# RMS norms of a two-layer decoder trunk on one core: from blocks between the matmul stages to steps streamed into them, the residual update on VectorE alone

## What is computed

```python
def rms_norm(x, g):
    y = x * lax.rsqrt(jnp.mean(x * x, axis=-1, keepdims=True) + RMS_EPS)
    return y * g

def decoder_layer(x, mem_kv, past, lp, rel_bias):
    g = lp['norm_g']
    mix, st = mixer_block(rms_norm(x, g[0]), lp, rel_bias, past)
    x = x + rms_norm(mix, g[1])
    x = x + rms_norm(cross_attention(rms_norm(x, g[2]), mem_kv, lp['w_xq'], lp['w_xo']), g[3])
    x = x + rms_norm(swiglu(rms_norm(x, g[4]), lp['w_ffn_in'], lp['w_ffn_out']), g[5])
    return x, st
```

## Time and profile before

| | |
|---|---|
| time, median of 3 executions | 3706.91 us (3703.59 to 3714.84) |
| profiled execution, its own time | 3719.7 us |
| its span, core 0 | 3717.9 us |
| mean granted TensorE clock | 0.812 |
| TensorE matmuls busy | 2937.5 us (79%) |
| TensorE weight loads busy | 2710.8 us (73%) |
| VectorE busy | 1452.8 us (39%) |
| ScalarE busy | 819.3 us (22%) |
| GpSimd busy | 353.1 us (9%) |
| HBM read / written | 385.95 / 19.55 MB, 109 GB/s over the span |

### The profile page before, as it was taken

One profiled execution on the slowest core, in us unless ns is written; L12 is line 12 of the kernel. 1 busy time (PEld: TensorE's weight loads), 2 busy tenths in 40 slices (PEclk: granted clock), 3 DMA queues, 4 the chain that ended last, 5 costly groups with the idle time before them and its releaser, 6 DMA issues. The chain is left out here.

```text
span 3717.9 us, 51710 instructions
## 1 busy us (share of the span) xinstructions
PE 2937.5 (79%) x19564; PEld 2710.8 (73%) x19564; DVE 1452.8 (39%) x3291; ACT 819.3 (22%) x1609; POOL 353.1 (9%) x344
## 2 busy tenths in 40 slices
PE   2798967469886797999939797865797867889997
PEld 1785656359885696999929665654697767879996
DVE  1225557315553313333122355762275332233322
ACT  0223311001222212222212232110122221222221
POOL 1000033230001001000010001324100010000000
PEclk8786789658996856999959778985598876689998
DMA  5221089443221401332113202956332140123331
GB/s 129 64 96 44 9 335 388 160 157 86 70 77 34 147 16 44 93 92 84 58 38 97 90 15 93 416 236 229 108 90 63 51 158 12 34 63 90 89 89 43
DMA packets 387293, 398.72 MB, mean 107 GB/s; under 512 B 47332, under 2 KB 350920, under 8 KB 370224
## 3 DMA queue, kind: packets, MB, share of 16 engines
q1 hardware_dynamic: 357888, 212.08, 19.6%
q0 software_dynamic: 29248, 184.63, 13.0%
HBM read 385.95 MB, written 19.55 MB: 109 GB/s over the span
## 5 line engine op out<-in xcount | busy, mean ns | idle before, releaser
L446 PE MATMUL pg<-act_hi,w_lo 128*128 128x260 f32 x3328 | 681.3, 286 | 116.4 <-PEq L149 43.7
L446 PE MATMUL pg<-act_hi,w_hi 128*128 128x260 f32 x3328 | 678.6, 286 | 0.0
L446 PE MATMUL pg<-act_lo,w_hi 128*128 128x260 f32 x3328 | 678.2, 286 | 0.0
L410 DVE TENSOR_TENSOR w_lo<-w_raw,w_hi 128x1024 fp32r<-128x1024 f32 x296 | 362.5, 1225 | 692.4 <-ACT w_hi L405 685.1
L446 PEld LDWEIGHTS pg<-act_hi,w_lo 128*128 128x128 f32 x3328 | 523.2, 192 | 121.4 <-issue 90.7
L446 PEld LDWEIGHTS pg<-act_hi,w_hi 128*128 128x128 f32 x3328 | 521.5, 191 | 0.0
L446 PEld LDWEIGHTS pg<-act_lo,w_hi 128*128 128x128 f32 x3328 | 520.8, 192 | 0.0
L405 ACT CAST w_hi<-w_raw 128x1024 fp32r<-128x1024 f32 x292 | 305.7, 1047 | 311.1 <-PE pg L446 140.1
L1240 PE MATMUL pg<-xt,w_raw 128*128 128x256 f32 x1024 | 243.7, 399 | 102.5 <-DVE xt L1303 102.5
L1240 PEld LDWEIGHTS pg<-xt,w_raw 128*128 128x128 f32 x1024 | 201.8, 200 | 141.6 <-DVE xt L1303 75.0
L1303 DVE STREAM_TRANSPOSE xt<-cache 128x256 f32<-128x256 f32 x512 | 180.8, 412 | 104.5 <-DMA cache<-in_cache_kv,gather_rows 104.3
(11 more groups left out here) (411 smaller groups left out, 3937.1 us busy)
## 6 DMA issues: line engine op xcount, KB each, us to landing
w_raw<-in_w_ffn_in SPq DMA_DIRECT2D x88, 512.0 KB, 3.8
w_raw<-in_w_in SPq DMA_DIRECT2D x80, 512.0 KB, 3.8
cmem<-in_cache_mem SPq DMA_DIRECT2D x16, 1024.0 KB, 14.2
w_raw<-in_w_ffn_out SPq DMA_DIRECT2D x32, 512.0 KB, 3.7
w_raw<-in_w_o SPq DMA_DIRECT2D x16, 512.0 KB, 3.7
w_raw<-in_w_xkv SPq DMA_DIRECT2D x16, 512.0 KB, 3.7
out_win_sample<-in_cache_win SPq DMA_DIRECT2D x2, 4088.0 KB
w_raw<-in_w_ffn_out SPq DMA_DIRECT2D x16, 384.0 KB, 3.2
```

What stands on the lines that cost most here:

```text
L410: e.tensor_tensor(w_lo[:, slot % 2, :], w_raw[:, slot, :], w_hi[:, slot % 2, :].bitcast(F32), ALU.subtract).then_inc(w_ready, 1)
L446: mm = e.matmul(pg[:, tslot, h, 0:wd], w[:, slot % 2, wk], x[:, k0 + k, at:at + wd], start=first and k == 0 and n == 0, stop=last and k == ...
```

## The change

- A norm's last factor, 1/rms of each token, is no longer multiplied into the operand of the next stage. It is a factor per column, so it is applied to the products: the operand is gain x `xT` alone, and VectorE multiplies each output tile by `rb`, a copy of the spread factor, when it empties PSUM (mixer, `ng`, merge gates, XQ, FFN-in).
- The squares for the norm after a sub-layer are made from PSUM as its output tiles come (`square_and_keep`), VectorE adds them up (`add_square`), and five small matmuls sum the total.
- The residual update (scale, add to `xT`, `act_lo` of the next operand) is done chunk by chunk on VectorE alone; ScalarE makes `act_hi` and the square of the new `xT`. GpSimd keeps the power.
- The next stage's first unit (XQ, FFN-in) runs chunk by chunk behind the update, and between its chunks TensorE sums the new squares with two float32 matmuls by `ones` (256 and 264 columns); the sums stand on all partitions, and `mean_square_dve` picks them off the diagonal.
- Norm 0 of layer 0 is done in a block ahead of the loop; for the next layer, the factor comes from the end of the FFN-out block. `norm_block` is gone.
- Blocks are merged: vector rows with mixer stage, WO with norms 1 and 2 and XQ, XO with norms 3 and 4 and FFN-in, FFN-out with norm 5. The ring's first four units are loaded ahead of the `cmp` weights. XKV moves into the LayerNorm block (units 44 to 51; OUT is 52, WO 60), with its operand prepared by VectorE in the gate stage's last three units. OUT and WO start when their operand's first chunk is split. Half of the `cache_mem` loads are issued in the WO block, half in the cross-attention block. A clear of the scope's semaphores moves to between cross attention and XO.

The diff, cut to what the prediction speaks of:

```diff
-U_MIX, U_MG, U_OUT, U_WO, U_XKV, U_XQ, U_XO, U_FI, U_FO, U_END = 0, 20, 44, 52, 60, 68, 72, 80, 124, 148
+U_MIX, U_MG, U_XKV, U_OUT, U_WO, U_XQ, U_XO, U_FI, U_FO, U_END = 0, 20, 44, 52, 60, 68, 72, 80, 124, 148
...
-        def norm_block(*norms):
...
+        def square_and_keep(e, n, u, m, dst, sq):
+            tile_done_(e, u)
+            if m >= 2:
+                e.wait_ge(acc_done, KC * n + m - 1)
+            elif n:
+                e.wait_ge(sq_used, KC * n)
+            e.activation(halves(sq[:, m % 2, :]), out_tile(m % 2), ACT.Square).then_inc(sq_ready, 1)
+            e.copy(halves(dst[:, m, :]), out_tile(m % 2)).then_inc(evac[m % 2], 1)
+        def add_square(e, n, m, sq, acc):
+            e.wait_ge(sq_ready, KC * n + m + 1)
+            if m == 0:
+                e.tensor_copy(acc, sq[:, 0, :]).then_inc(acc_done, 1)
+            else:
+                e.wait_ge(acc_done, KC * n + m)
+                e.tensor_tensor(acc, acc, sq[:, m % 2, :], ALU.add).then_inc(acc_done, 1)
...
+        def total_pe(e, n, acc):
+            e.wait_ge(acc_done, KC * n + KC)
+            for tt in range(5):
+                w = P if tt < 4 else NB
+                mm = e.matmul(pa[0][0:w, tt:tt + 1], acc[:, tt * P:tt * P + w], ones[:, 0:1], start=True, stop=True)
+            mm.then_inc(tot_mm, 1)
...
+        def keep_rb(e, n, i):
+            e.wait_ge(rstd_bc, i + 1)
+            e.copy(halves(rb[:]), pn[:, :, 0:HALF]).then_inc(rb_ready, 1)
...
+        def scaled_dve(e, n, c, B):
+            if c >= 4 and c % 2:
+                e.wait_ge(x_odd, 4 * n + (c - 4) // 2 + 1)
...
+            e.scalar_tensor_tensor(halves(B.t[:, c % 4, :]), halves(B.Y[:, c, :]), gain(2 * n + 1, c), pn[:, :, 0:HALF],
+                                   ALU.mult, ALU.mult).then_inc(t_ready, 1)
...
+        def add_x(e, n, c, B):
+            e.wait_ge(t_ready, KC * n + c + 1)
+            e.tensor_tensor(xT[:, c, :], xT[:, c, :], B.t[:, c % 4, :], ALU.add).then_inc(x_odd if c % 2 else x_even, 1)
...
+        def lo_dve(e, i, c):
+            e.wait_ge(hi_ready, KC * i + c + 1)
+            e.scalar_tensor_tensor(act_lo[:, c, :], xT[:, c, :], gain(2 * i, c), act_hi[:, c, :].bitcast(F32), ALU.mult, ALU.subtract
+                                   ).then_inc(lo_ready, 1)
...
+        def update_dve(e, n, B):
+            e.wait_ge(rstd_bc, 2 * n + 1)
+            scaled_dve(e, n, 0, B)
+            for c in range(KC):
+                if c + 1 < KC:
+                    scaled_dve(e, n, c + 1, B)
+                add_x(e, n, c, B)
+                if n < 2 and c:
+                    lo_dve(e, n + 1, c - 1)
+            if n < 2:
+                lo_dve(e, n + 1, KC - 1)
...
+        def update_act(e, n, B):
+            for c in range(KC):
+                e.wait_ge(x_odd if c % 2 else x_even, 4 * n + c // 2 + 1)
+                if n < 2:
+                    e.activation(act_hi[:, c, :], xT[:, c, :], ACT.Copy, scale=gain(2 * n + 2, c)).then_inc(hi_ready, 1)
+                if c >= 2:
+                    e.wait_ge(sq_used, KC * n + c - 1)
+                else:
+                    e.wait_ge(acc_done, KC * n + KC)
+                e.activation(B.sq[:, c % 2, :], xT[:, c, :], ACT.Square).then_inc(xsq_ready, 1)
...
+        def sum_squares(e, n, c, sq):
+            e.wait_ge(xsq_ready, KC * n + c + 1)
+            e.matmul(pa[0][:, 0:SPLIT], ones[:], sq[:, c % 2, 0:SPLIT], start=c == 0, stop=c == KC - 1)
+            e.matmul(pa[1][:, 0:TOK - SPLIT], ones[:], sq[:, c % 2, SPLIT:TOK], start=c == 0, stop=c == KC - 1).then_inc(sq_used, 1)
...
+        def mean_square_dve(e, n):
+            e.wait_ge(sq_used, KC * n + KC)
+            for t in range(5):
+                w = P if t < 4 else NB
+                src = pa[t // 2][0:w, (t % 2) * P:(t % 2) * P + w] if t < 4 else pa[1][0:NB, SPLIT:SPLIT + NB]
+                dve_chain(e, e.tensor_tensor_reduce(extract[0:w, 0:w], src, ident[0:w, 0:w], 1.0, 0.0, ALU.mult, ALU.add, ms[0:w, t:t + 1]))
+            e.tensor_scalar(ms[:], ms[:], 1.0 / D_MODEL, RMS_EPS, ALU.mult, ALU.add).then_inc(ms_ready, 1)
...
+        def first_stage(e, u0, n, i, sq):
+            await_(e, w_ready, u0 + 1)
+            await_(e, evac[0], u0 // 2)
+            for k in range(KC):
+                operand_ready(e, i, k)
+                wk = slice(k * P, (k + 1) * P)
+                for x, (w, v) in enumerate(((w_lo, act_hi), (w_hi, act_lo), (w_hi, act_hi))):
+                    for h in range(2):
+                        mm = e.matmul(pg[:, 0, h, 0:HALF], w[:, 0, wk], v[:, k, h * HALF:(h + 1) * HALF],
+                                      start=k == 0 and x == 0, stop=k == KC - 1 and x == 2)
+                if k == KC - 1:
+                    mm.then_inc(unit_done, 1)
+                sum_squares(e, n, k, sq)
...
+                        weights(e, U_MIX, RING, mix_parts)
...
-                        weights(e, U_MIX, RING, mix_parts)
...
+                            e.tensor_tensor(halves(to), out_tile(s % 2), halves(rb[:]), ALU.mult).then_inc(evac[s % 2], 1)
...
+                        e.tensor_tensor(halves(th[:]), pn[0:NG_W, :, 0:HALF], halves(rb[0:NG_W, :]), ALU.mult).then_inc(ng_sc, 1)
...
-            norm_block((0, xT, True))
...
+                        plain_stage(e, U_MIX, 20, (act_hi, act_lo), ready=lambda k: operand_ready(e, 0, k))
...
+                    e.dma_start(mem_f.rearrange("p c m -> p (c m)"), mem_dram.ap()).then_inc(mem_in, 16)
...
-                    tile_done_(e, U_MG + RING * j + s)
-                    e.activation(halves(G[:, bass.ds(RING * j + s, 1), :].rearrange("p o t -> p (o t)")), out_tile(s % 2), ACT.Tanh,
-                                 scale=0.5).then_inc(evac[s % 2], 1)
+                    u = RING * j + s
+                    await_(e, evac[s % 2], U_MG // 2 + 2 * j + s // 2 + 1)
+                    e.activation(G[:, bass.ds(u, 1), :].rearrange("p o t -> p (o t)"), sq_c[:, s % 2, :], ACT.Tanh, scale=0.5).then_inc(g_done, 1)
...
+                    if u >= 21:
+                        e.wait_ge(mem_in, 16)
+                        for c in range(3 * (u - 21), min(3 * (u - 21) + 3, KC)):
+                            link(e.tensor_scalar(mem_f[:, c, :], mem_f[:, c, :], vecs[:, V_MEM + c:V_MEM + c + 1], None, ALU.mult))
+                            link(e.tensor_copy(mem_hi[:, c, :], mem_f[:, c, :]))
+                            e.tensor_tensor(mem_lo[:, c, :], mem_f[:, c, :], mem_hi[:, c, :].bitcast(F32), ALU.subtract).then_inc(mem_set, 1)
+                    tile_done_(e, U_MG + u)
+                    if u >= 2:
+                        e.wait_ge(g_done, u - 1)
+                    e.tensor_tensor(halves(sq_c[:, s % 2, :]), out_tile(s % 2), halves(rb[:]), ALU.mult).then_inc(evac[s % 2], 1)
...
+                        e.wait_ge(mem_set, KC)
+                        unit(0)
+                        unit(1)
...
+                                if lead and s == 0:
+                                    e.wait_ge(op_lo, k + 1)
...
-                norm_block((1, Y, False), (2, xT, True))
...
+                        for m in range(KC):
+                            split_hi(e, U_WO + m + 1, (m + 1) % RING, landed(U_WO + m + 1))
+                            square_and_keep(e, 0, U_WO + m, m, bufs.Y, bufs.sq)
...
+                        split_hi(e, U_XQ + 1, 1, landed(U_XQ + 1))
+                        update_act(e, 0, bufs)
+                        split_hi(e, U_XQ + 2, 2, landed(U_XQ + 2))
+                        keep_rb(e, 0, 1)
...
+                            split_lo(e, U_WO + m + 1, (m + 1) % RING)
+                            add_square(e, 0, m, bufs.sq, bufs.acc)
+                        split_lo(e, U_XQ + 1, 1)
+                        total_dve(e, 0)
+                        diag_dve(e, 0, bufs.diag)
+                        update_dve(e, 0, bufs)
+                        mean_square_dve(e, 0)
+                        split_lo(e, U_XQ + 2, 2)
+                        diag_dve(e, 1, bufs.diag)
...
+                        total_pe(e, 0, bufs.acc)
+                        spread_pe(e, 0, bufs.diag)
+                        first_stage(e, U_XQ, 0, 1, bufs.sq)
+                        for s in range(1, XH):
+                            products(e, U_XQ + s, s, U_XQ // 2 + s // 2, s % 2, 0, KC, (act_hi, act_lo), True, True, (HALF, HALF))
+                            if s == 1:
+                                spread_pe(e, 1, bufs.diag)
...
-                norm_block((3, Y, False), (4, xT, True))
...
+                def fi_act(e, j, s):
+                    f = 2 * j + s // 2
+                    if s % 2 == 0:
+                        await_(e, evac[0], U_FI // 2 + f + 1)
+                        e.activation(thf[:, s // 2, :], gs[:, s // 2, :], ACT.Tanh, scale=0.5).then_inc(th_f, 1)
+                    else:
+                        await_(e, t2_f, f + 1)
```

(40 more changed lines are left out.)

592 lines of the change are left out of this document (342 added, 250 removed).

## The result

The changed kernel takes 3517.18 us (median of 4, 3512.53 to 3522.04) against 3705.25 us (3701.97 to 3714.84) for the one before: ratio 0.9489, 95% interval 0.9464 to 0.9513. The forecast was 3487 in a range of 3432 to 3550. The median fell by 188 us and the profiled span by 197.6 (3717.9 to 3520.3); 219.6 were forecast. (The two differ since the profiled execution of before, 3719.7 us, lay further above its median than that of the changed kernel, 3522.04.)

What follows compares the result with a forecast made beforehand. TensorE was taken to bound the gate stage and FFN-in, waiting chains the rest; savings of 121.0 us (layer 0) and 122.6 (layer 1) less 24.0 once gave 219.6, hence 3487 against the median of 3706.9, range 3432 to 3550.

Steps and rivals of the forecast that it cites:

- Layer start: Vector rows to first mixer matmul: that matmul comes at +14.5 us, saving 43.9 us in layer 0, 45.5 in layer 1.
- WO's end to cross attention: Last WO matmul to cross attention: with the update streamed by chunk, 125.4 us become 48.5, saving 76.9 per layer.
- Block ahead of the loop: First norm's factor computed once ahead of the layer loop: costs 24.0 us once.
- Gate stage: Merge gates: a VectorE and ScalarE loop takes 6.83 us per unit against 5.77, costing 24.7 us per layer.
- Rival 1: Gate stage stays TensorE's, VectorE having 36 us to spare: 2 x 27.2 us come back, 3433 us; chance 0.10.
- LN block and OUT's start: LayerNorm block, taking in XKV, costs 12.4 us per layer; OUT and WO, starting at one chunk, save 9.0 together.
- rival 5: First units don't really stream, chunk waits opening late: four units of 5.8 us later, 3510 us; chance 0.02.
- FFN-in: XO's end to FFN-in's unit 2 saves 36.1 us; two added multiplies per pair cost 0, 5.65 us against 5.77.
- Rival 3: FFN-in's loop exceeds the unit that covers it by 0.5 us per pair: 3509 us; chance 0.13.
- Rival 2: TensorE works the new streamed parts at its lower clock level: 80 us more, 3567 us; chance 0.09.
- Rival 4: FFN-in pauses each unit for VectorE's multiply, TensorE's clock falls and stays low: 429 us more, 3916 us; chance 0.04.
- XO's eight squares: XO stage: each unit gains a square of 0.64 us, half should hide, costing 2.2 us per layer.

Runs made afterwards that it cites:

- the last run: Changed kernel with silu and gate multiply moved earlier and OUT's block wait removed, plus unread TensorE filler matmuls: 3414.47 us (without the fillers 3433.95).

## Why the prediction was right, and where it was wrong

- *Layer start* (43.9 and 45.5; measured 45.4 and 45.3) and *WO's end to cross attention* (76.9; 76.3 and 78.1): right, and together more than the whole net gain. Inside the second, sizes were off and offset each other. A chunk of the update takes VectorE 1.95 us, not 2.1 (its adds start at 1154.66, 1156.61, 1158.56), since successive instructions overlap by some 0.08 us. TensorE was not always ahead of that pace: its first two chunks, at the lower level, took 2.80 and 2.72 us (they start at 1156.17, 1158.97 and 1161.69), and the later ones 1.60, so that from the fourth chunk on it is TensorE that sets the pace. The second factor's power took 2.54 us instead of 1.64, which cost nothing, as the run with the split moved shows.
- *Block ahead of the loop*: 20.0 instead of 24.0. TensorE reached the upper level within the fourth chunk (75.95), and the sums behind it took about 0.9 to 1.0 us per chunk instead of 1.75; the reductions were shorter than the 0.42 taken (0.29 and 0.08, overlapping, 0.33 from one to the next).
- *Gate stage*: the loop of 6.83 us was right (6.80), and so was taking over the occupancy. Rival 1, and with it the forecast by occupancy that the prediction made from the Trainium skill's "Perfetto Trace Analysis", section "Identifying the Most-Contended Engine", fell in the changed kernel: TensorE still has the highest busy time, 146.28 us, but of 164.6. With the multiply moved, the stage comes within 3.7 us of the 141.1 that this rival gave it, with as much work on VectorE. Busy time says what an order can reach; the order says what this one reaches.
- *LN block and OUT's start*: wrong by 6.1 and 7.6. "Now for one chunk, about 1.4" failed for OUT: a wait was added and the older, stronger one stayed in a helper that the diff does not show. That is rival 5's mechanism, though at OUT, where it was not priced; 4.3 per layer are shown by the run without it. WO did start by chunk (4.7 and 5.4 in the table), and XQ and FFN-in did stream. Of what is left, 1.8 in layer 0 and 3.3 in layer 1, 1.8 is a mean that took 3.81 us where 2.0 was taken: TensorE had idled 4.06 us ahead of it and ran it at granted clock 0.50, while before it had idled 0.95 us and took 1.99 at 1.00.
- *FFN-in*: wrong by 15.0 and 13.6. The failed step is "5.65 < 5.77, the unit that covers it". The 5.65 were nearly right (5.56), but the loop also holds the way from TensorE's last matmul to VectorE (1507.7, estimated as the unit's start plus 5.77, to 1508.34) and from the split to the next matmul (1501.62 to 1501.91), 0.9 us together. Rival 3, priced at 0.5 per pair, came true at 12.13 - 11.54 = 0.59. What the forecast took for the likelier case did not hold; a margin of 0.12 out of terms rounded to 0.1 was no margin.
- *Rival 2* (the lower level in streamed parts) held for the first chunks only: the streamed stretch ran at 0.93, and what the last run gains with fillers there and at the mixer's starts is at most its 19.5 us, not 80. *Rival 4* did not occur: FFN-in paused once per pair and stayed at 1.00.
- *Small sums and signs.* Three sums are not what their terms give: the first mixer matmul at +14.5 (the terms give 14.3; it came at 12.8 and 14.4), the +4.0 ahead of the power (the lengths named give 3.2; it took 3.6), and XO's eight squares of which half should hide (2.6, not 2.2; 1.9 and 1.4 were lost). GpSimd was not "below 20 us in powers" but at 24.9: four of its 13 powers took 2.54 us beside VectorE's split.
- *Where luck helped.* The two terms that fell short cost 42.3 us in the two layers together, yet the sum missed by 22.0 only. The other 20.3 were not foreseen: 9.0 at the end of the layers, which no run takes apart, 4.0 at the block ahead of the loop, 11.5 at cross attention less 8.3 in the table's row with the cache attention, both of which differ between executions, and small rests. Without them the time would still have been in the range (3487 + 42 = 3529), but not as near to the forecast.

## What to carry to other kernels

When work is added to an engine with time to spare, write out the order in which that engine and its partner wait, from matmul's end to next matmul's start, with each hand-over; an order that puts the tile's evacuation behind work nobody waits for makes a loop longer than the matmuls that should cover it. A finer wait is worth nothing while the coarse one stands, so look for the coarse one in the helpers that call the changed code. Where a transition is a chain of short steps, it is worth trying to fill TensorE's idle time with matmuls that nobody reads: here the granted clock then stayed at 1.00.
